# First block's attention: where the squares of a pair's second query tile are totalled

## The reference, cut to what matters

```python
q = rms_norm(aq.reshape(B, L, ATT_HEADS, ATT_HEAD_DIM), q_norm_g)   # 16 heads of 64
k = rms_norm(ak.reshape(B, L, ATT_KV_HEADS, ATT_HEAD_DIM), k_norm_g) # 2 heads of 64
q = apply_partial_rope(q, cos, sin)                                  # first 16 of 64
k = apply_partial_rope(k, cos, sin)
ya = sliding_window_sink_attention(q, k, v, sink).reshape(B, L, ATT_WIDTH)
ya = ya * jax.nn.silu(ag)
```

## Time and profile before

| | |
|---|---|
| median of 3 runs | 3007.18 us (3005.82 to 3008.84) |
| the profiled execution | 3007.3 us, of which the span is 3005.5 |
| PE busy | 2895.2 us, 96% |
| DVE busy | 1626.0 us, 54% |
| ACT busy | 1257.8 us, 42% |
| POOL busy | 190.1 us, 6% |
| mean granted TensorE clock | 0.992 |
| layer 0's steps 4 to 8 | about 110 to 149 us of the span |
| layer 1's | about 690 to 729 us |

### The profile page before, as it was taken

How to read it: one execution, slowest core, us unless ns; L and a number is a source line. 1 busy time by engine, 2 the same in 40 slices (tenths; PEclk the granted TensorE clock), 3 DMA queues, 4 the chain that set the end, 5 groups by cost and what they waited for, 6 DMA issues and landing times.

```text
span 3005.5 us, 42406 instructions
## 1 busy us (share of the span) xinstructions
PE 2895.2 (96%) x17134; PEld 2479.8 (83%) x17134; DVE 1626.0 (54%) x3223; ACT 1257.8 (42%) x2630; POOL 190.1 (6%) x207
## 2 busy tenths in 40 slices
PE   8899999999999999999999999999999999999998
PEld 6888888988877777898888888887898888888886
DVE  6766645366665454676433564336676433565334
ACT  5455523255554233565334333223565324433222
POOL 2100000020000000100000000000100000000000
PEclk9999999999999999999999999999999999999999
DMA  3111321211113222322232222333322232222222
GB/s 116 52 46 52 107 69 64 92 53 59 52 52 114 69 94 89 109 75 78 84 119 89 73 78 79 97 100 104 116 72 80 84 113 85 82 73 88 95 91 85
DMA packets 99726, 250.07 MB, mean 83 GB/s; under 512 B 8597, under 2 KB 44845, under 8 KB 99274
## 3 DMA queue, kind: packets, MB, share of 16 engines
q1 hardware_dynamic: 99530, 247.35, 25.3%
HBM read 239.60 MB, written 6.50 MB: 82 GB/s over the span
## 4 chain that ended last, share of the span: by engine, by line
PE 79%; DVE 10%; ACT 6%; issue 2%; DMA 1%; POOL 1%; SPq 0%; DVEq 0%; POOLq 0%; ACTq 0%
PE ps L93 76%; PE ps L96 3%; ACT Z L99 3%; DVE Z L110 2%; DVE Z L102 2%; DVE cl L102 1%; ACT ch L99 1%; DMA st<-in_stream_dram 1%; POOL stat L102 1%; DVE stat L123 1%; DVE ZR L102 1%; DVE Z L106 1%; DVE stat L110 1%; ACT ZR L99 1%; DVE Z L120 0%
## 5 line engine op out<-in xcount | busy, mean ns | idle before, releaser
L93 PE MATMUL ps<-hl,ch 128*128 128x512 f32 (+1 forms) x2512 | 830.3, 359 | 0.0
L93 PE MATMUL ps<-hh,ch 128*128 128x512 f32 (+1 forms) x2368 | 801.4, 365 | 27.2 <-ACT Z L99 13.0
L102 DVE TENSOR_TENSOR cl<-st,ch 128x1024 fp32r<-128x1024 f32 (+1 forms) x436 | 501.1, 1156 | 569.5 <-ACT ch L99 568.4
L93 PE MATMUL ps<-hh,cl 128*128 128x512 f32 (+1 forms) x2368 | 791.4, 361 | 0.0
L99 ACT ACTIVATE ch<-st 128x1024 fp32r<-128x1024 f32 (+1 forms) x436 | 428.6, 990 | 343.7 <-PE ps L93 305.2
L93 PEld LDWEIGHTS ps<-hh,ch 128*128 128x128 f32 x2368 | 421.9, 189 | 110.1 <-ACT Z L99 19.6
L93 PEld LDWEIGHTS ps<-hl,ch 128*128 128x128 f32 x2512 | 447.6, 190 | 72.4
L93 PEld LDWEIGHTS ps<-hh,cl 128*128 128x128 f32 x2368 | 422.9, 190 | 70.5
L99 ACT ACTIVATE Z<-ps 128x512 f32<-128x512 f32 (+7 forms) x506 | 216.5, 437 | 569.7 <-PE ps L93 462.8
L93 PE MATMUL ps<-ZR,ch 128*128 128x512 f32 (+2 forms) x1680 | 437.2, 350 | 2.0 <-DVE cl L102 1.6
L93 PEld LDWEIGHTS ps<-ZR,ch 128*128 128x128 f32 x1680 | 284.2, 189 | 47.4 <-issue 3.9
(11 more groups left out here) (134 smaller groups left out, 3158.6 us busy)
## 6 DMA issues: line engine op xcount, KB each, us to landing
st<-in_stream_dram SPq DMA_DIRECT2D x372, 512.0 KB, 3.4
st<-in_stream_dram SPq DMA_DIRECT2D x64, 256.0 KB, 3.2
Z<-decay_rows SPq DMA_DIRECT2D x8, 904.0 KB, 5.6
Z<-bias_lines SPq DMA_DIRECT2D x16, 448.0 KB, 3.5
ya_spill<-Z SPq DMA_DIRECT2D x8, 512.0 KB, 4.0
Z<-ya_spill SPq DMA_DIRECT2D x2, 2048.0 KB, 7.5
Z<-in_x_dram SPq DMA_DIRECT2D x4, 512.0 KB, 5.7
Z<-in_mem_dram SPq DMA_DIRECT2D x2, 1024.0 KB, 6.6
```

The source lines that it names most:

```text
L93: return Ins(self, self.e and self.e.matmul(o, a, b, start=start, stop=stop, skip_group_check=True))
L102: return Ins(self, self.e and self.e.tensor_tensor(o, a, b, op))
```

## The change

In steps 6, 14 and 22 of each layer, `qsum` of the pair's second tile (3, 5 or 7) is put ahead of that step's `sA` and no longer behind it. The new function `early` puts it for each tile in `st["turn"]` that is at its first stage, and sets the tile aside in `st["summed"]`; the step's `chain()` then gives the other tile its `rope` and takes the tile back for its next stage, so that `rope` and `ropeq` of both tiles stay in the steps where they were. On POOL, the power of tile 3 now stands ahead of the cosine product of tile 2.

```diff
-        st = {"conv": None, "turn": []}
+        st = {"conv": None, "turn": [], "summed": []}
...
                 if x < (1 if t == 8 else 2):
                     st["turn"].append((t, n, x + 1))
+            st["turn"] += st["summed"]
+            st["summed"] = []
+
+        def early():
+
+            keep = []
+            for t, n, x in st["turn"]:
+                if x == 0 and t < 8:
+                    put("qsum", l, t, n)
+                    st["summed"].append((t, n, 1))
+                else:
+                    keep.append((t, n, x))
+            st["turn"] = keep
...
         for s in range(35):
+            if s in (6, 14, 22):
+                early()
             if s < 32:
                 put("sA", l, s)
```

## The result

The changed kernel took 2985.09 us (median of 4 runs, 2981.35 to 2989.01) against 3008.01 (4 runs, 3005.82 to 3010.58): ratio 0.9924, 95% interval 0.9906 to 0.9941, a gain of 22.9 us. Its profiled execution is the fastest of the four, 2981.35 us with a span of 2979.6; that of before had 3005.5. So the two profiles differ by 25.9 us, three more than the medians do. Forecast were 2988 us and a gain of 19.4.

A forecast was written before the change was run, and what follows sets the result against it. TensorE, busy 96% of the span, was taken as the bound, so only faster matmuls or fewer waits help. 15.2 + 5.7 - 0.3 - 1.2 = 19.4 us off 3007.3 gave 2988 us, range 2983 to 2997.

The forecast's parts named there:

- The six waits: TensorE's waits for DVE's copy of the sums in steps 6, 14, 22 of each layer go: 15.2 us gained.
- The low clock: Four stretches at about 0.64 granted clock behind four of those waits return to 1.00: 5.7 us gained.
- DVE's and POOL's side: POOL's second product, now directly behind the first, delays DVE's softmax step: 0.2 us per pair, 1.2 us lost.
- the cover: DVE's idle time before splitting the turned probabilities, 1.05 us left after the change; lateness beyond it reaches TensorE.
- The new wait at the sums: TensorE's sums, now ahead of the scores, wait for their bank in layer 1: 0.1 us each, 0.3 lost.
- (a): Rival: the waits go, but the low clock moves to other waits; 2993.6 us, chance 0.15.
- (b): Rival: POOL's products hold DVE twice a pair, 9.3 us lost instead of 1.2; 2996.0 us, chance 0.14.
- (c): Rival: POOL's power also holds DVE, delaying step 8's scores; 3007 us, no change; chance 0.06 together with (e).
- (d): Rival: as (c), with POOL's power also stretched by DVE; slower, 3013.3 us, chance 0.03.
- (e): Rival: something else in DVE's queue keeps the bank from freeing sooner; 3007 us; chance 0.06 together with (c).

The follow-up runs named there:

- e3: Kernel before, with DVE's copy and POOL's power of the second tile moved early, TensorE's sums left behind the scores: 2992.82 us, ratio 0.9943.
- e4: Kernel before, with only TensorE's sums moved ahead of the scores, DVE's copy and POOL's power left late: 3011.33 us, ratio 1.0004.
- e1: Kernel before, with the change made only in step 6 of each layer (first pair): 3002.03 us, ratio 0.9973.
- e2: Kernel before, with the change made only in steps 14 and 22 of each layer: 2994.77 us, ratio 0.9949.
- e5: The changed kernel run again, unaltered, beside the kernel before: 2986.2 us, ratio 0.9926.
- e6: Changed kernel, but POOL's power of the second tile stays behind the first tile's cosine product: 2988.63 us, ratio 0.9934.
- e8: Changed kernel, plus first rotated tile's halves ahead of the scores of steps 7, 15, 23, and tile 1's squares totalled before the step loop: 2984.3 us, ratio 0.9921.

## Why the prediction was right

**The six waits (15.2 us): right.** They are gone, and e3 and e4 show that it is DVE's copy and not the sums. The term was a little small, by a margin around each wait that the sum left at nothing. From the first instruction behind the value product to the scores of step 8, the first pair took 147.97 - 130.49 = 17.48 us and takes 145.12 - 130.24 = 14.88: 2.60 us saved for a wait of 2.24. The matmul before the wait ended, as the profile models it, 0.15 us after its successor could have started (the last one starts at 135.22, one step of 0.12 later is 135.34, and the wait is counted from 137.73 - 2.24 = 135.49), and the first matmul behind the wait is followed after 0.23 instead of 0.12 us. These two make 0.26 of the 0.36 us. Over six pairs such margins are about 2 us, an estimate.

**The low clock (5.7 us): right in its sum, wrong in its reason.** I took the four stretches as bound to the four waits, and named waits of 2.4 to 2.7 us as what went before each fall; the wait of 2.73 us at 717.50, with no fall behind it, already stood against that. e1 and e2 show that waits of one length have the low clock or not. What the change does is to take six waits out of those that can bring it.

How much that is where the waits stood, the starts of the scores tell. Each pair has a stretch from the scores of step 4, 12 or 20 to those of step 8, 16 or 24. For layer 0's second pair it is, before and after, 37.69 and 33.58 us:

```profile
175.04 0.30 PE L93 MATMUL ps<-mskb,idb 128*128 128x144 bf16 x2 [0.32 <-ACT Z L99]
212.73 0.28 PE L93 MATMUL ps<-mskb,idb 128*128 128x144 bf16 x2 [0.63 <-issue]
...
172.22 0.30 PE L93 MATMUL ps<-mskb,idb 128*128 128x144 bf16 x2 [0.32 <-ACT Z L99]
205.80 0.29 PE L93 MATMUL ps<-mskb,idb 128*128 128x144 bf16 x2 [0.77 <-issue]
```

The six together take 223.3 us in the kernel before and 200.9 and 201.1 in the two profiles of the changed kernel: 22.4 and 22.2 us less, nearly the whole gain of the medians. The waits and what is said of steps 8, 16 and 24 below make 15.2 - 0.3 of it, the four low stretches 5.7, the margins the remaining 1.8. The same sum gives 215.1 us for e1 and 209.8 for e2, that is 8.2 and 13.5 us less than before, against 7.6 and 14.8 of the medians: e1 loses two low stretches, e2 gains two. How many of the six have one in other executions, no profile shows.

For the program as a whole the clock's part is less certain. The mean granted clock of the timed executions is 0.990 over the 18 and 9 of the kernel before that ran beside the experiments, and 0.993 over the 9 of the changed kernel. At a clock of 0.5, a difference of 0.003 is 0.003 x 3000 / 0.5 = 18 us less of it. The four windows behind the waits had means of 0.64, 0.66, 0.61 and 0.64 over 4.3 to 4.4 us, which is 12.6 us at 0.5, and cost 5.7 us, 0.45 for one; by that, 18 us are worth some 8 us; the single executions of the kernel before, where 0.001 of clock goes with about 1 us, would make it 3. By these estimates the clock's part lies at 3 to 8 us. How it splits up outside of the six stretches stays open.

**DVE's and POOL's side (1.2 us): the mechanism right, the size too large.** The first product fitted into DVE's idle time as forecast, and the second held the scalings (not the sum) for 0.84 us, within the cover. The waits ahead of steps 8, 16 and 24 went from 0.69, 0.63, 0.70, 0.43, 0.39 and 0.44 us to 0.69, 0.77, 0.81, 0.43, 0.42 and 0.45: 0.3 us in all. The cover was real: e3 overdrew it, and its six waits are 0.4 to 0.8 us longer each.

**The new wait at the sums (0.3 us): not there.** No wait of 0.25 us or more stands ahead of the sums in any of the six.

**The rivals.** (a) needed the low clock to move to other places; it does, in part, from execution to execution: in e5's profile 34.1 us of it are left of 41.0, though the 12.6 us behind the four waits are gone. (b), two operations of DVE held per pair, is what e3 shows (16.8 us gained instead of 22.9), not the change itself. (c) and (d) needed the power to hold DVE, and the one-column operations at 133.03 run inside of a power at full speed. The Trainium skill ("SBUF — State Buffer", § Who interferes with whom) would have the power keep them out like the products, as a GpSimd instruction that reads SBUF; the trace agrees for the products, with operations of DVE that have two inputs in SBUF (1.09 us and 1.34 us above), and not for the power. The scalings, which took 1.47 us, read one tensor there, and that part of the rule doesn't speak of them. What the power does show is the other half of the rule: at 76.68 it takes 2.87 us instead of 1.95, and this split of DVE is under way as it comes:

```profile
76.52 1.22 DVE L102 TENSOR_TENSOR cl<-st,ch 128x1024 fp32r<-128x1024 f32 x1
```

(e) is out: the waits went.

The gain of 22.9 us is then 15.2 of waits, about 2 of margins around them, less 0.3, and a rest of 6 us, which fits the 5.7 of the four low stretches. The forecast of 19.4 was 3.5 low, by the margins (1.8 in the stretches), by DVE's side (1.2 instead of 0.3), by the wait at the sums (0.3 instead of nothing) and by 0.5 that lies outside of the stretches.

## What to carry to other kernels

A PSUM bank of such a ring stays taken until it is copied out, not until its matmuls end: where a short copy stands in an engine's queue behind a long dependent chain, the next user of the ring waits for the chain. Moving ten small matmuls and a copy of 0.16 us by one place in the order was worth 23 us. Before such a move, ask of each engine that takes part what it is moved past: on TensorE it gained nothing by itself (e4) but spared DVE a wait of 1.75 us for sums that come late (e3), on DVE it was the gain, on POOL it made 1 to 2 us in the pairs (e6) and took away the further gain ahead of step 0 (e8), where the instruction it overtook was wanted at once.

## What the runs showed of the hardware

- A wait of TensorE of 1.7 to 2.7 us was followed by a stretch with a granted clock of 0.61 to 0.67 (a mix of 1.2 and 2.4 GHz) in some places and by 1.00 in others, for the same code: in e1 at 262 and 773 us, not at 198 and 838. A wait of 2.0 us at the same place of the same kernel had 1.00 behind it in one execution and 0.53 in another (64.4 us in the changed kernel's first profile, 65.3 in e5's). Such a wait costs its length, or its length and 1.4 us (37.69 against 36.25 us for one stretch with a wait of 2.38, before and in e1).
- POOL's cosine product (128x528, 1.3 us) held DVE's scaling (128x272), its sum of two columns and its one-column operation until it was over (1.47 for two scalings instead of 0.63, 1.34 instead of 0.16, 1.09 for two instead of 0.35). Its power on 128x10 (1.95 us) didn't hold the one-column operations that came inside of it (at 133.03 in the changed kernel, at 133.38 in e6).
